# Two weight units of the last expert, each sent as sixteen transfers of eight partitions

## What is computed

```python
x = x + pool_mixer(...); x = x + swiglu(rms_norm(x), ffn_w1, ffn_w3, ffn_w2)       # layer 0
k, v = shared_kv(rms_norm(x))
x = x + swa_sink_attention(rms_norm(x), k, v, ...)                                # layer 1
for e in range(8):                                                                 # top 2 of 8 experts
    y = y + combine[:, e:e + 1] * ((silu(h @ w1[e]) * (h @ w3[e])) @ w2[e])
x = x + y; out = rms_norm(x)
```

## Time and profile before

| what | value |
|---|---|
| median of three runs | 1180.82 us |
| profiled execution, its span from the first to the last instruction | 1179.2 us |
| PE busy | 1101.2 us (93%) |
| chain that ended last | PE 66%, DMA of the expert weights 30% |
| read from HBM | 414.09 MB |
| mean granted clock of TensorE | 0.985 |

### The profile page before, as it was taken

One profiled execution on the slowest core, in us unless ns is written; L12 is line 12 of the kernel. 1 busy time (PEld: TensorE's weight loads), 2 busy tenths in 40 slices (PEclk: granted clock), 3 DMA queues, 4 the chain that ended last, 5 costly groups with the idle time before them and its releaser, 6 DMA issues.

```text
span 1179.2 us, 25221 instructions
## 1 busy us (share of the span) xinstructions
PE 1101.2 (93%) x11793; PEld 651.2 (55%) x11793; DVE 320.1 (27%) x434; ACT 197.2 (17%) x280; POOL 40.7 (3%) x36
## 2 busy tenths in 40 slices
PE   7999999999999999999989969999997789999775
PEld 6888888888863357563347315444732444464233
DVE  3654454458761030021021002202200220022023
ACT  5544443446630000000000000000000000000002
POOL 3000000002100000000000000000000000000000
PEclk9999999999999999999999999999999899999988
DMA  9985555543469999999999999999999999999993
GB/s 345 388 289 179 191 197 183 180 160 126 148 267 399 417 376 424 428 421 425 426 427 420 426 427 421 425 425 427 423 425 426 425 423 425 426 421 425 427 424 138
DMA packets 58129, 417.87 MB, mean 354 GB/s; under 512 B 5682, under 2 KB 11876, under 8 KB 33444
## 3 DMA queue, kind: packets, MB, share of 16 engines
q1 hardware_dynamic: 54608, 410.05, 85.4%
q0 software_dynamic: 1440, 4.46, 1.0%
q10 hardware_dynamic: 1972, 1.70, 0.5%
HBM read 414.09 MB, written 2.10 MB: 353 GB/s over the span
## 4 chain that ended last, share of the span: by engine, by line
PE 66%; DMA 30%; DVE 2%; ACT 1%; SPq 0%; issue 0%; ACTq 0%; DVEq 0%
DMA weights<-in_moe_w 30%; PE psum L842 20%; PE psum L875 16%; PE psum L742 8%; PE psum L744 8%; PE psum L743 8%; DVE hid_t L1671 1%; PE psum L750 1%; DVE sil L1669 1%; PE psum L958 1%; PE psum L821 1%; PE psum L811 1%; DMA consts<-in_table 0%; PE psum L1079 0%; PE psum L857 0%
## 5 line engine op out<-in xcount | busy, mean ns | idle before, releaser
L842 PE MATMUL psum<-weights,xg 128*32 128x512 f32 (+1 forms) x5072 | 493.1, 547 | 46.7 <-DMA weights<-in_moe_w 46.7
L842 PEld LDWEIGHTS psum<-weights,xg 128*32 128x32 f32 x5072 | 184.3, 111 | 352.8 <-issue 306.4
L875 PE MATMUL psum<-weights,hid_t 128*32 128x256 f32 x4480 | 250.7, 380 | 12.1 <-DVE hid_t L1671 8.4
L875 PEld LDWEIGHTS psum<-weights,hid_t 128*32 128x32 f32 x4480 | 168.1, 110 | 91.3 <-issue 18.4
L1669 DVE TENSOR_TENSOR sil<-sil,psum 128x1536 f32<-128x1536 f32 (+3 forms) x16 | 21.1, 1320 | 492.3 <-PE psum L842 491.6
L1532 DVE TENSOR_TENSOR low<-raw,high 128x2048 fp32r<-128x2048 f32 x50 | 114.6, 2292 | 85.5 <-ACT high L1242 85.3
L1242 ACT ACTIVATE high<-raw 128x2048 fp32r<-128x2048 f32 x51 | 97.8, 1918 | 81.9 <-PE psum L744 81.2
L742 PE MATMUL psum<-high,a_hi 128*128 128x512 f32 x224 | 87.3, 390 | 0.9 <-DVE a_lo L1569 0.9
L744 PE MATMUL psum<-low,a_hi 128*128 128x512 f32 x224 | 87.2, 389 | 0.0
L743 PE MATMUL psum<-high,a_lo 128*128 128x512 f32 x224 | 87.1, 389 | 0.0
L1298 ACT ACTIVATE y_hi<-psum 128x768 fp32r<-128x768 f32 (+1 forms) x7 | 5.0, 719 | 490.7 <-PE psum L875 490.7
(11 more groups left out here) (243 smaller groups left out, 636.8 us busy)
## 6 DMA issues: line engine op xcount, KB each, us to landing
weights<-in_moe_w SPq DMA_DIRECT2D x128, 1792.0 KB, 35.2
weights<-in_moe_w SPq DMA_DIRECT2D x48, 2048.0 KB, 37.5
raw<-in_ffn_w SPq DMA_DIRECT2D x42, 1024.0 KB, 6.7
weights<-in_moe_w SPq DMA_DIRECT2D x16, 1024.0 KB, 37.3
raw<-in_w_q SPq DMA_DIRECT2D x4, 1024.0 KB, 5.2
raw<-in_w_o SPq DMA_DIRECT2D x4, 1024.0 KB, 4.9
x_res<-in_x SPq DMA_DIRECT2D x2, 512.0 KB, 5.3
raw<-in_pool_w SPq DMA_DIRECT2D x1, 1024.0 KB, 10.8
```

Source lines behind the costliest of these rows:

```text
L842: mm = pe.matmul(UP[c][g * BLK:(g + 1) * BLK, r, :], xg[:, k_, r * BLK:(r + 1) * BLK], w[:, g], start=k_ == 0, stop=k_ == DT - 1)
L875: mm = pe.matmul(Y[g * BLK:(g + 1) * BLK, r, :], hid_t[c][:, r, at_:at_ + BLK], w[:, b, g * GW:(g + 1) * GW], start=i == 0 and b == 0 and ...
```

## The change

For the last expert of the first pass, units 4 (of w1) and 12 (of w3) are no longer one DMA of 128 partitions but sixteen DMAs of eight partitions each. The i-th of them carries partitions i, i + 16, ..., i + 112. Each adds 16 to a semaphore of the unit's own, and PE waits for 256 on that one. The bytes, their places in SBUF and the order of the units are the same. In the two further passes the count waited for on `moe_landed[4]` and `moe_landed[12]` is 16 lower, since the last expert of the first pass no longer adds to them.

```diff
+STRIPED = (4, 12)
+STRIPES = 16
@@ semaphores
+        striped_landed = {j: sem(f"striped_landed{j}") for j in STRIPED}
@@ class Pass
+            def striped(self, j, e):
+                return not self.block and e == E - 1 and j in STRIPED
+            def landed_unit(self, j, e):
+                return self.landed(e) - 16 if self.block and j in STRIPED else self.landed(e)
@@ expert_loads (SP)
-                    if j < MU - 1:
+                    if ps.striped(j, e):
+                        cols = slice(0, moe_size(j))
+                        for i in range(STRIPES):
+                            sp.dma_start(expert_tile(ps, j, e, cols)[i::STRIPES],
+                                         expert_source(who, *key, cols)[i::STRIPES]).then_inc(striped_landed[j], 16)
+                    elif j < MU - 1:
@@ expert_feed_forward (PE)
-                    pe.wait_ge(moe_landed[j], ps.landed(e))
+                    if ps.striped(j, e):
+                        pe.wait_ge(striped_landed[j], 16 * STRIPES)
+                    else:
+                        pe.wait_ge(moe_landed[j], ps.landed_unit(j, e))
```

## The result

The changed kernel takes 1226.34 us (median of four runs, 1225.63 to 1227.04) against 1180.97 us for the kernel before in the same comparison: the ratio is 1.0386, interval 1.0374 to 1.0398, 45.4 us slower. The profiled span is 1225.2 us. The sign was foretold; the size was more than double the forecast of 20.4 us.

The account below looks back on a forecast made before the run. Weight DMAs at full engine pace bound the kernel: +34.6 us of stripe work, less 13 us lead and 1.2 us absorbed, gives +20.4 us, 1180.82 to 1201.2 us. Its own range was 1192 to 1210, for all cases 1177 to 1208.

Parts of the forecast that it names:

- What bounds the kernel: Expert stage: weight DMAs run at the full pace of sixteen engines, 425 GB/s, so the last bytes' landing counts.
- The spread: Striped units: the same eight engines, called carriers, bring sixteen rows each, 8.64 us instead of 4.32; the others skip.
- Issuing and increments: SP's 32 issues, about 6 us a unit, are covered and cost nothing; thirty extra increments per carrying engine cost 0.2 us.
- Issues of several microseconds: Sign in SP's stripe line: a full queue, then starvation of the other engines, unpriced; 0.3 to 0.9 us expected.
- The destination, the price per row: Stripe writes into partitions other engines fill: rows take two to three times 0.54 us; chance 0.58.
- The middle between double and triple: Price of both striped units on the engines carrying them: +34.6 us, between +25.9 and +43.2.
- a carrier that enters the partitions of a late engine, which is never idle, makes two: Stripe writes: two engines meeting take twice as long per row; a second carrier at the same group makes three.
- the 13 us in hand: End of the expert stage: half the engines finish 13 us early; if these carry the stripes, 13 us is subtracted.
- 34.6 - 13 - 1.2: Forecast sum: extra stripe work, less the early engines' lead, less 1.2 us absorbed before PE's end: +20.4 us.
- Free destinations: Rival at the stripe writes: rows keep 0.54 us, early engines carry them; 2.2 us gained, 1178.6 us; chance 0.32.
- No spread change: Rival: eight-row transfers are cut finer and take all sixteen engines, only issues move; 1180.8 us; chance 0.04.
- The carriers are the late half: Rival: the engines bringing the stripes finish last, +8.64 us with free destinations, 1189.5 us; chance 0.06.

Follow-up runs that it names:

- m1_alone: Separate load-only kernel: three 128-row units, then two units in another form, nothing behind; 32.8 us for rows sixteen apart, 16.7 us for sixteen-partition transfers.
- cols16: Changed kernel, but each of the sixteen transfers takes all 128 partitions and a sixteenth of the columns: 1181.89 us, ratio 1.0011.
- m2_mixed: Separate load-only kernel: three ordinary units, one unit in another form, three ordinary units behind; 52.3 us with partitions sixteen apart, 33.0 with half a unit in lower partitions.
- m3_two: Separate load-only kernel: two engines carry sixteen rows each, ordinary units behind; 36.6 us in lower partitions, 45.0 in two foreign groups, 54.5 both in one group.
- drop_upper: Changed kernel, but units 4 and 12 load only the lower 64 partitions, as eight transfers of every fourth of 32: 1180.15 us, ratio 0.9998.
- four: Changed kernel, but each of the sixteen transfers takes every fourth of 32 partitions: 1209.82 us, ratio 1.0247.
- sixteen: Changed kernel, but units 4 and 12 go as eight transfers of sixteen partitions, every eighth: 1203.74 us, ratio 1.0196.
- near_src: Changed kernel, but each transfer reads rows of eight neighbouring partitions in HBM and writes the same places in SBUF: 1225.76 us, ratio 1.0381.

## Why the prediction was right and wrong

**What bounds the kernel.** Right. In the last expert every wait of PE but the 0.94 us for `hid_t` ends with a weight DMA, and PE's end and the last landing both came some 46 us later (1213.05 for 1166.98; about 1210 for 1164).

**The spread.** Right: the share of 0.50 in m1_alone. Eight rows, eight engines, the same eight each time. That was the rule of the Trainium skill that the prediction named, and the runs bear out this part of it; that they are the lowest-numbered ones no run here shows.

**Issuing and increments.** Right in the sum. Issues of several microseconds did appear, a sign that the prediction listed as a starving queue; in the changed kernel the share near 1.00 shows that nothing starved. In cols16, with as many transfers, half of the engines did run dry for some 8 us, and the lead covered it: 1.4 us were left.

**The destination, the price per row.** The shared destination was the right choice. The middle between double and triple was too high for the kernel: 215 to 226 GB/s are double. Tripling, 155 GB/s, came only with all engines abreast (m2_mixed).

**The step that failed: "a carrier that enters the partitions of a late engine, which is never idle, makes two", and by the sum nobody else is touched.** The sum charged only the carriers. The runs show that all sixteen go at half pace while a foreign group is written (m3_two: two writers, 210 GB/s for everybody). So the time in which the early carriers pass their stripes is lost for the late engines too: 1065 to 1085, 20 us at half pace, 10 us lost for a unit. The sum had no such term; it is 20 us for both units.

**The term that was mis-sized with it: the 13 us in hand.** For the stripes it measured zero, because two of the carriers are late themselves (drop_upper, the share of 0.13 at the end): they begin their stripes after the others are through, in the second stretch, with sixteen rows at double time, 17.3 us in place of 4.3, 13.0 more. Per unit that is 10 + 13.0 = 23, for both 46. Measured are 21.3 and 22.3 for one and 45.4 for both. In the forecast's terms: it had 34.6 - 13 - 1.2; the runs show 26.0 (double, not the middle), nothing in hand, and 20 for the late engines. The split is seen in the trace of the changed kernel: unit 3, ahead of the stripes, lands 10.5 us late, unit 4 another 12.6, and the next pair gives 10.0 and 12.8. `four` and `sixteen` give 30.2 and 22.5 by the same account with their stretches as measured, against 29.3 and 22.9; with stretches of 8.6 us, as taken before those runs, it gave 25.8 and 17. The half pace, the two late carriers and the landings are measured. No run takes one of the two terms away without the other.

**The rivals.** Free destinations: out, by m1_alone and near_src. No spread change: out, by the share of 0.50. "The carriers are the late half": held to be 0.06, true for two of eight. It was put as all or nothing; the case in between, which was the one, was not among the rivals. The split into halves by the share at the end tells how many engines are late, not which.

What stays open: why a writer in a foreign group slows engines whose groups nobody else touches. The Trainium skill, "DMA: Bandwidth & Descriptors", under back-pressure in remote DMA, says that a saturated destination port of SBUF clogs the path back to the DMA engines that write it and to any that share that path. The page says this of transfers between cores. The 210 GB/s of m3_two would fit it for plain loads from HBM, the 302 with both writers in one group less well, and no run here looks inside the path. Nor is it shown what made the late half late, or which engines they are.

## What to carry to other kernels

Of the forms measured here a load is fastest when each DMA engine writes the partitions that a 128-partition transfer gives it. Before some of the engines are given more work, measure with one stage alone which engines a shape takes and where they write; the DMA share against the rate tells both, and a share of 1 with half the rate is the sign of engines in each other's way, while a share of a half with half the rate is the sign of engines that stand idle. A lead of some engines at the end covers idle time of their own (cols16). It is worth nothing if the change slows all of them, or if one of those that get the work is not ahead.

## What the hardware showed that was not expected

Two engines writing one row each into groups of other engines took the whole core from 424 to 210 GB/s (m3_two). Sixteen engines on rows eight apart moved 211 GB/s instead of 425 (m1_alone). An issue of an eight-partition transfer with a run-time address took 0.596 us at the median in the changed kernel, one of 128 partitions 0.333 in the kernel before. It is not the eight partitions as such: in m1_alone, with fixed addresses, eight partitions sixteen apart in SBUF took 0.563 us at the median and eight neighbouring ones 0.295.
